# Second attention's output projection: float32 products replaced by three fp32r products on split operands

## What is computed

```
def mla_attention(xn, positions, k, v, w_dq, cq_norm, w_uq, w_o):
    c_q = rmsnorm(xn @ w_dq, cq_norm)
    q = (c_q @ w_uq).reshape(B, S, MLA_HEADS, MLA_NOPE + MLA_ROPE)
    ...
    o = causal_block_attention(q, k, v, 1.0 / math.sqrt(MLA_NOPE + MLA_ROPE))
    return o.reshape(B, S, MLA_HEADS * MLA_V) @ w_o
```

## Time and profile before

| | |
|---|---|
| median of 3 runs | 1819.31 us (1817.47 to 1821.43) |
| the profiled execution, its own time | 1820.8 us |
| its span | 1818.7 us |
| mean granted PE clock | 0.96 |
| PE busy | 1647.0 us, 91% of the span |
| DVE busy | 1072.1 us, 59% |
| ACT busy | 566.0 us, 31% |

### The profile page before, as it was taken

How to read it: one execution, slowest core, us unless ns; L and a number is a source line. 1 busy time by engine, 2 the same in 40 slices (tenths; PEclk the granted TensorE clock), 3 DMA queues, 4 the chain that set the end, 5 groups by cost and what they waited for, 6 DMA issues and landing times.

```text
span 1818.7 us, 22755 instructions
## 1 busy us (share of the span) xinstructions
PE 1647.0 (91%) x7883; PEld 1171.8 (64%) x7883; DVE 1072.1 (59%) x2454; ACT 566.0 (31%) x1111; POOL 348.4 (19%) x296
## 2 busy tenths in 40 slices
PE   7999999999999998999999999798797788888877
PEld 5888999868689995884664796444343344434333
DVE  6556555546455553546444642777777777666765
ACT  2544444335344441424110431122221222222222
POOL 3550000000000000000000000454434444443540
PEclk9999999999999998999999999799999989998989
DMA  6635566323466652522405340899999999999997
GB/s 210 187 93 162 170 187 198 133 61 99 153 181 186 198 153 67 162 95 92 185 24 185 139 151 27 353 420 421 421 421 422 421 421 421 421 421 421 422 420 297
DMA packets 205769, 437.43 MB, mean 241 GB/s; under 512 B 10608, under 2 KB 136976, under 8 KB 171792
## 3 DMA queue, kind: packets, MB, share of 16 engines
q0 software_dynamic: 36864, 268.45, 35.5%
q1 hardware_dynamic: 168848, 168.20, 28.8%
HBM read 435.54 MB, written 1.05 MB: 240 GB/s over the span
## 4 chain that ended last, share of the span: by engine, by line
PE 71%; DMA 16%; DVE 8%; issue 3%; ACT 1%; SPq 0%; POOL 0%; DVEq 0%; another core or an unknown queue 0%; ACTq 0%
PE ps L553 33%; DMA OT<-in_peer_uv,IX 13%; PE ps L1438 13%; PE ps L745 6%; PE ps L1229 3%; PE ps L1086 3%; PE ps L1099 3%; PE ps L720 2%; PE ps L584 2%; DMA SLOT<-in_peer_uv,IX 2%; DVE SLOT L2761 2%; PE ps L559 1%; PE ps L629 1%; DMA SLOT<-in_fox_w_in 1%; PE ps L1178 1%
## 5 line engine op out<-in xcount | busy, mean ns | idle before, releaser
L1944 POOL DMA_INDIRECT SLOT<-in_peer_uv,IX x128 | 138.5, 1082 | 1272.3 <-DVE IX L2755 1025.2
L1438 PE MATMUL ps<-SLOT,AR 128*128 128x512 f32 x512 | 267.2, 679 | 92.9 <-ACT AR L1862 92.9
L553 PE MATMUL ps<-ARH 128*128 128x256 f32 (+1 forms) x2248 | 298.8, 285 | 0.0
L553 PEld LDWEIGHTS ps<-ARH 128*128 128x128 f32 x2248 | 285.1, 191 | 3.8 <-issue 0.5
L1438 PEld LDWEIGHTS ps<-SLOT,AR 128*128 128x128 f32 x512 | 109.5, 219 | 244.2 <-issue 131.4
L2761 DVE SCALAR_TENSOR_TENSOR SLOT<-SLOT,V 128x1024 f32<-128x1024 f32 x128 | 153.1, 1224 | 74.5 <-DMA SLOT<-in_peer_uv,IX 72.5
L2078 DVE TENSOR_TENSOR ARH<-SLOT,ARH 128x2048 fp32r<-128x2048 f32 (+1 forms) x88 | 154.1, 1756 | 50.9 <-ACT ARH L1521 34.1
L1438 PE MATMUL ps<-AR 128*128 128x512 f32 x320 | 144.2, 600 | 8.3 <-ACT AR L1862 8.3
L1856 ACT ACTIVATE AR<-AR 128x4 f32<-128x4 f32 (+1 forms) x66 | 13.6, 205 | 370.4 <-DVE SLOT L2761 184.5
L745 PE MATMUL ps<-ARH 128*128 128x512 f32 x528 | 123.8, 390 | 0.0
L1438 PEld LDWEIGHTS ps<-AR 128*128 128x128 f32 x320 | 60.3, 192 | 81.8 <-issue 64.7
(11 more groups left out here) (424 smaller groups left out, 2611.1 us busy)
## 6 DMA issues: line engine op xcount, KB each, us to landing
SLOT<-in_w_gate SPq DMA_DIRECT2D x44, 512.0 KB, 4.0
SLOT<-in_w_up SPq DMA_DIRECT2D x44, 512.0 KB, 5.3
SLOT<-in_w_down SPq DMA_DIRECT2D x44, 512.0 KB, 5.2
SLOT<-in_w_in SPq DMA_DIRECT2D x9, 2048.0 KB, 8.2
SLOT<-in_fox_w_in SPq DMA_DIRECT2D x16, 512.0 KB
SLOT<-in_w_ckv SPq DMA_DIRECT2D x4, 2048.0 KB, 8.7
XT<-in_w_pq_by_head SPq DMA_DIRECT2D x8, 1024.0 KB
SLOT<-in_w_uq_by_pair SPq DMA_DIRECT2D x8, 768.0 KB, 4.8
```

The lines of the kernel that those rows point to most:

```text
L553: m = pe.matmul(outp, l, r, start=(n_ == 0), stop=(n_ == len(pairs) - 1))
L1438: m = pe.matmul(ps[:, b, :], DIAG[:, j, :], v_row(j)[:, c * 512:(c + 1) * 512], start=False, stop=closing)
L1944: pool.indirect_dma_start(PAIR[j], None, pairs, bass.IndirectOffsetOnAxis(IX[:, t, j:j + 1], 0)).then_inc(gathered[j], 16)
```

## The change

The eight chunks of the output and both halves of `w_o` are split into high and low, and the 32 float32 products become 96 fp32r products. On ACT `out_turned` takes the place of `ot_copy`: it writes the high half and no longer frees bank 2. On DVE `out_low(i - 1)` subtracts the high half from bank 2 and frees the bank; it stands after `attend_tail(i)`. `high_out` and `low_out` split the weight in halves of 4 chunks: SLOT2's on ACT after the rounds of pairs 5 and 6, on DVE before the scores of pair 7; SLOT3's after the last transposed output. On PE `out_part` does all products, and waits for each half of the weight.

```diff
-            two_tiles(a["mla_w_o"][0])
+            two_tiles(a["mla_w_o"][0], arrival=raw_here)
...
-            def out_part(t, ks):
+            def out_part(t, ks, c=0):
+                b = (6, 2)[c] + t
+                s = 2 + c
                 if ks[0] == 0:
-                    take(6 + t)
+                    take(b)
                 for k in ks:
-                    m = pe.matmul(ps[:, 6 + t, :], cols(OT, t, k), slot(2, KC, 512)[:, k, :], start=(k == 0), stop=(k == KC - 1))
-                    if k < KC - 1:
-                        first(m)
+                    if t == 0 and k % 4 == 0:
+                        pe.wait_ge(split[s], T.next(split[s]))
+                    w = (O_HIGH[s][k // 4][:, k % 4, :], low_of(s, KC, 512)[:, k, :])
+                    for n_, (l, r) in enumerate(thirds(lambda h: cols(O2HL[h], t, k), lambda h: w[h])):
+                        m = pe.matmul(ps[:, b, :], l, r, start=(k == 0 and n_ == 0), stop=(k == KC - 1 and n_ == 2))
...
                 m.then_inc(full["a"][2], 1)
-                T.add(free["a"][2])
+                T.add(free["v"][2])
...
             mla_scores(PAIRS - 1)
-            pe.wait_ge(here[2], T.next(here[2], 16))
             out_part(0, range(PAIRS - 2))
...
-            row_tile(3, (2, 3), OT)
+            for t in range(NT):
+                out_part(t, range(KC), 1)
+            release(3)
...
+            def high_out(s, q):
+                if q == 0:
+                    act.wait_ge(raw_here[s], T.next(raw_here[s], 16))
+                act.copy(O_HIGH[s][q], chunks(SLOT[s], q)).then_inc(sem("high_ready"), 1)
+            def out_turned(i):
+                act.wait_ge(full["a"][2], T.next(full["a"][2]))
+                act.copy(O2HL[0][:, ds(i, 1), :].rearrange("p o s -> p (o s)"), ps[:, 2, 0:S]).then_inc(sem("ot_high"), 1)
...
             mla_round(PAIRS - 4, 3)
+            high_out(2, 0)
             mla_round(PAIRS - 3)
+            high_out(2, 1)
             two_probs()
             turned_probs()
-            ot_copy(PAIRS - 2)
-            ot_copy(PAIRS - 1)
+            out_turned(PAIRS - 2)
+            out_turned(PAIRS - 1)
+            high_out(3, 0)
+            high_out(3, 1)
...
+            def low_out(s, q):
+                dve.wait_ge(sem("high_ready"), T.next(sem("high_ready")))
+                low(chunks(SLOTR[s], q), chunks(SLOT[s], q), O_HIGH[s][q]).then_inc(split[s], 1)
+            def out_low(i):
+                dve.wait_ge(sem("ot_high"), T.next(sem("ot_high")))
+                one = ds(i, 1)
+                TT(O2HL[1][:, one, :].rearrange("p o s -> p (o s)"), ps[:, 2, 0:S], O2HL[0][:, one, :].rearrange("p o s -> p (o s)").bitcast(F32),
+                   ALU.subtract).then_inc(free["v"][2], 1)
```

More of the change, by code:

```diff
@@ L217, in program @@
         CQHL = (halves(13408, 6, S), halves(7424, 6, S))
+        flat = lambda x: x[:].rearrange("p a b -> p (a b)")
+        O_HIGH = {2: [view(flat(x), 4, 512) for x in (XTR, XT2R)], 3: [halves(9216, 4, 512), halves(11264, 4, 512)]}
+        O2HL = (OTR, view(SLOTR[1][:, 2048:4096], KC, S))
         CKT = arena(12896, 2, S)
@@ L641, in out_proj @@
                     row_tile(2 + c, (2 * c, 2 * c + 1), X)
-            def out_part(t, ks):
+            def out_part(t, ks, c=0):
+                b = (6, 2)[c] + t
+                s = 2 + c
                 if ks[0] == 0:
-                    take(6 + t)
+                    take(b)
                 for k in ks:
-                    m = pe.matmul(ps[:, 6 + t, :], cols(OT, t, k), slot(2, KC, 512)[:, k, :], start=(k == 0), stop=(k == KC - 1))
-                    if k < KC - 1:
-                        first(m)
+                    if t == 0 and k % 4 == 0:
[3 more added lines that the diff above has]
+                        m = pe.matmul(ps[:, b, :], l, r, start=(k == 0 and n_ == 0), stop=(k == KC - 1 and n_ == 2))
+                        if k < KC - 1:
+                            first(m)
                 if ks[-1] == KC - 1:
-                    m.then_inc(full["v"][6 + t], 1)
-                    T.add(free["v"][6 + t])
+                    m.then_inc(full["v"][b], 1)
+                    T.add(free["v"][b])
             def qk_part(s_):
@@ L1659, in mla_round @@
                 turned_probs()
-                ot_copy(i)
+                out_turned(i)
             with T.loop("mla", PAIRS // 2 - 2) as i:
@@ L2309, in _, with mla_round @@
             rotate()
-            def mla_round(s=None):
+            def low_out(s, q):
[6 more added lines that the diff above has]
+                   ALU.subtract).then_inc(free["v"][2], 1)
+                T.add(free["v"][2])
+            def mla_round(i, s=None):
                 mla_scores()
@@ L2315, in mla_round @@
                 rotate()
[L2316 to L2321, removed]
+                attend_tail(i)
+                out_low(i - 1)
+            mla_scores()
+            low_queries(0)
+            rotate()
+            attend_tail(0)
+            with T.loop("mla", PAIRS // 2 - 2) as i:
+                mla_round(i * 2 + 1, 3)
+                mla_round(i * 2 + 2, 0)
+            mla_round(PAIRS - 3, 3)
+            mla_round(PAIRS - 2)
+            low_out(2, 0)
+            low_out(2, 1)
             mla_scores()
             attend_tail(PAIRS - 1)
+            out_low(PAIRS - 2)
+            out_low(PAIRS - 1)
+            low_out(3, 0)
+            low_out(3, 1)
             first_gu()
@@ L2863 @@
     "pe:ffn0": dict(gu_split0=1, free_v4=1, gu_split1=1, free_v5=1, dn_split0=1, dn_split1=1),
-    "pe:mla": dict(free_v1=2, free_v2=2, slot_here1=32, free_a6=2, pair_split=1, free_v0=2, probs_ready=4, free_a3=2, free_a4=2,
-        free_a2=2, free_v5=2, split3=1),
+    "pe:mla": dict(free_v1=2, free_v2=4, slot_here1=32, free_a6=2, pair_split=1, free_v0=2, probs_ready=4, free_a3=2, free_a4=2,
+        free_v5=2, split3=1),
     "pe:ffn1": dict(gu_split0=1, free_v4=1, gu_split1=1, free_v5=1, dn_split0=1, dn_split1=1),
@@ L2878 @@
     "dve:ffn0": dict(silu_ready=2, dve_chain=4, free_v4=1, high_ready=4, free_v5=1),
-    "dve:mla": dict(full_v1=2, free_v1=2, full_v2=2, free_v2=2, high_ready=2, full_v0=2, free_v0=2, probs_ready=4, dve_chain=2,
-        full_v5=2, free_v5=2),
+    "dve:mla": dict(full_v1=2, free_v1=2, full_v2=2, free_v2=4, high_ready=2, full_v0=2, free_v0=2, probs_ready=4, dve_chain=2,
+        full_v5=2, free_v5=2, ot_high=2),
     "dve:ffn1": dict(silu_ready=2, dve_chain=4, free_v4=1, high_ready=4, free_v5=1),
```

## The result

The changed kernel takes 1824.57 us (median of 20 runs, 1819.52 to 1833.44); the kernel before, timed beside it, 1819.31 (20 runs, 1817.34 to 1824.45). The ratio is 1.0034, 95% interval 1.0024 to 1.0044: slower by 6.2 us (4.4 to 8.0) by the ratio, by 5.3 by the medians. The prediction was 1824.8, slower by 5.5.

A forecast was written before the change was run, and what follows sets the result against it. PE was taken as the bound. Bank 2's wait 4.9, the last round 0.0 and the clock 0.6 summed to +5.5 us, 1824.8 on the median; the forecast's own range was 1822.2 to 1827, the whole range 1817.5 to 1828.8.

The forecast's parts named there:

- The products: All 32 output products on PE: 27.8 us before, 22.4 after as fp32r matmuls 0.233 apart, 5.4 us less PE work.
- The rival with 0.216: Matmul pitch 0.216 on PE: 75 matmuls behind the late flips save 1.3 us more, 1823.5 us; chance 0.04.
- The wait for bank 2: In the rounds, second scores wait for `out_low` on DVE: 3 x 1.10 plus 2 x 0.79, 4.9 us; bounds 3.4 to 6.6.
- The rival in which the loop's wait is hidden: No cost from bank 2 in the rounds, only the last round's 0.0 left: 1819.3 us, not slower; chance 0.13.
- The last round: From pair 7's scores to SLOT3's end: 5.4 saved, 1.1 + 1.6 + 0.5 + 2.2 lost, net 0.0; bounds -2.2 to +1.5.
- the second rival: The last round's split waits vanish or halve, loop as forecast: +1.1 us, 1820.4; chance 0.11.
- the third rival: Loop's wait hidden and split waits gone or halved: -3.8 to -5.4 us, about 1815; chance 0.06.
- DVE's cover: Before the last residual: DVE's residual steps end at 500.9, before PE's products at 501.5, a cover of 0.6 us.
- What was costed at nothing: SLOT2's high half on ACT may wait for its transfer; flips coming 1.1 later cover it, otherwise 1.85 us once.
- The clock: Half clock on PE behind the last round's new idle stretches: entered as 0.6 us, between nothing and 3.4 for both.
- The rival with falls at both gaps: Clock falls at both new gaps, or in the rounds too: 4.9 + 3.4 = +8.3 us, 1827.6; chance 0.16.
- The prediction's sign of being wrong: Wrong if second scores start without a wait, splits finish before PE asks, or the last round's clock is well below 1.

The follow-up runs named there:

- the best version: Changed kernel with transposes of pairs 0 to 5 in bank 7, SLOT2's and SLOT3's splits earlier, `out_low` behind the next scores on DVE: 1814.15 us, ratio 0.9968.
- the wait-alone kernel: Kernel before, still with float32 products and no split, but bank 2 freed by a DVE copy behind `attend_tail` instead of ACT's copy: 1824.93 us, ratio 1.0025.
- the other-bank kernel: Changed kernel with the transposes of pairs 0 to 5 in bank 7, those of pairs 6 and 7 still in bank 2: 1822.60 us, ratio 1.0012.

## Why the prediction held, and where not

The sum was 4.9 + 0.0 + 0.6 = 5.5; measured are 5.3 by the medians and 6.2 by the ratio. The mechanisms were all found in the trace; the total agrees better than its terms do, so that it came this close is in part luck.

- **The products** (5.4 less PE work, 0.233 apart). Right. SLOT3's 48 take from 492.51 to 503.95, 11.4 us, against 13.90; SLOT2's first 21 are 0.23 apart; the best version gets 5.0 from them. The rival with 0.216 falls. The chain of the prediction itself saves about 5.2 and not 5.4 on PE in the last round, and has 0.3 and not 0.5 at the flips; its list of terms is rounded where its times are not, and the net is the same. The Trainium skill ("TensorE: Matmul & The Clock Gate", Wait — 56ns, not 53.3ns?) has 215.7 ns for 512 columns at the full clock and 426.7 at half: the second agrees with the 0.43 here, the first is below the averages of these products, 0.227 (20 starts from 476.88 to 481.19) and 0.233 (SLOT3's).
- **The wait for bank 2.** The mechanism, its place and its count of rounds were right, and the wait-alone kernel shows it by itself. **The term was mis-sized**: 4.9 for five scores, measured 3.7 (0.64 to 0.81 each). `attend_tail` and `out_low` took their 0.78 and 0.41; what was too high is the restart, 0.34 from the earlier trace rows where 0.06 is seen, in all six rounds. With 0.06 the sum would have been 3.5. The lower bound, 3.4, was made with 0.04. PE was busy 93% of the rounds where 88% was forecast. The step took a price from a release whose surroundings differ: the same 0.33 stands behind the same rotation in the other-bank kernel (432.88 + 0.68 to 433.89). In the code five more waits stand on PE between the one for the bank that the rotation frees and the matmul (in `evacuated(0, 6)` and `take(1)`, each for DVE's and ACT's count of a bank), and one behind the wait for bank 2. That this makes the difference is not tested, and it can't be all: the products behind a split have no such wait, and start 0.15 behind DVE's low half (474.14 + 2.28 to 476.57). The rival in which the loop's wait is hidden falls.
- **The last round** (0.0). Where the clock stays it is -0.5. The waits were 0.8 before the scores (predicted 1.1), 1.37 for SLOT2 (1.6), 0.4 at the flips (0.5) and 1.92 for SLOT3 (2.2): each a little smaller. For the scores and the two splits the reason is the same, a restart of 0.06 and 0.15 instead of 0.34. That the splits' waits vanish or are halved, the second rival, did not happen. What the third rival put at about 1815, both the loop's wait and the splits' gone, came only when the order was changed for it: the best version, 1814.15.
- **DVE's cover.** 0.6 us were left between DVE's last work and the residual. There was none: from 495.47 on DVE had no idle time before the last residual at 504.00, and PE's last matmul ended at 503.95. The two engines end together, so this cost nothing, but a shorter PE alone would have brought nothing either; with SLOT3's split earlier DVE waited for PE again, 1.34.
- **What was costed at nothing.** SLOT2's high half waited 3.3 us on ACT for its transfer and made PE wait for nothing, as said.
- **The clock** (0.6, from the earlier trace rows). Right in kind, small in size: one gap costs 1.5 us in four of six profiles, 1.0 on average. The loss within the stage is 3.2 or 4.7. The rival with falls at both gaps was seen in none. The prediction's sign of being wrong, a clock well below 1 in the last round, came in no clear form: 1.00 in the first profile, 0.95 in two of those with a fall.

Two errors of opposite sign, 1.2 too much for the bank and about 0.4 too little for the clock, and 0.5 in the last round, leave a stage of about +4.2; the whole time rose by 5.3 to 6.2. Another 0.4 lies outside of the span: an execution's own time is 2.44 to 2.58 us above its span in every run of the kernels that have the split operands, and 2.06 to 2.19 in every run of before and of the wait alone; what takes it isn't shown. The 0.7 to 1.6 us that are left, and the runs up to 1833 us, which no profile caught, stay open. The six runs of the changed kernel above 1829 us had a mean granted clock of 0.956 to 0.961, the ten below 1824 one of 0.961 to 0.963, so the clock in other stages is the first thing to look at.

## What to carry to other kernels

When a copy that frees a buffer grows a second step on another engine, the buffer stays taken until that engine's order reaches it: look up who takes the buffer next before counting what the faster products save. Here the saving was real and 5 us, the wait for a bank and two splits placed too late ate all of it and more, and moving the same instructions to a free bank and to earlier places gave it back. Take the price of a restart from a wait with the same surroundings. Before explaining a difference between two profiles, compare the granted clock behind the same waits in both. And if two engines end a stage together, expect a gain on one of them alone to stop short.

## What the runs showed of the hardware

- Waits of PE of 1.37 and 1.92 us amid dense work, behind which the granted clock fell in four of six profiles, and never behind both; where it fell, seven or so matmuls of 128x512 started 0.43 apart instead of 0.23. The same kernel's stage therefore has two lengths, 80.9 and 82.4 to 82.5.
- The wait of PE for the norm behind the stage, 2.86 to 2.94 us in every profile, was followed by a granted clock of 0.57, 1.00 or 0.50 in the three windows above; the 32 small matmuls behind it took 5.46 us in the kernel before and 3.84 in the changed kernel's first profile.
- The granted clock can fall while the records show PE busy without a gap. The 64 narrow float32 matmuls further behind the attention, with the same code and count, take 17.47 or 20.82 us, and the longer ones ran in part at half clock; that is the step from 308 to 311 us named above. Timeline and window of PE, of the kernel before and then of the changed kernel profiled again:

```profile
816.84 17.47 PE L553 MATMUL ps<-SLOT,XT 128*128 128x8 f32 x64
```

```profile
816.84:824.84 8.00, 8.00 (x44) 5.61 (x43) 4.48 (x13) 5.37 (x5) 0.00 (x0) 1.00 0.74 264
```

```profile
820.35 20.82 PE L556 MATMUL ps<-SLOT,XT 128*128 128x8 f32 x64
```

```profile
820.35:828.35 8.00, 8.00 (x38) 5.93 (x37) 4.56 (x13) 5.38 (x5) 0.00 (x0) 0.66 0.75 263
```

- PE started 0.06 us after DVE's release of bank 2, behind which one more wait follows in its code, 0.33 after the rotation's release of bank 0, behind which five follow, and 0.15 after a split's low half, behind which none follows. Why is not shown.
